# One hybrid decoder layer on one core: queries scaled by minus one eighth on eviction, row minima for row maxima, and a low part cut in eight pieces

## The reference, cut to what matters

```python
    s_own = jnp.einsum('hqd,hld->hql', q_c, k_own).astype(f32) * scale     # scale = ATT_HEAD ** -0.5 = 1/8
    s_own = jnp.where(k_pos[None, None, :] <= q_pos[None, :, None], s_own, NEG_INF)
    p = jax.nn.softmax(jnp.concatenate([s_sel, s_own], axis=-1), axis=-1).astype(v_own.dtype)
...
    merged = (g_a * jnp.einsum('bsc,cd->bsd', y_a, w_br_rwkv[l])
              + g_b * jnp.einsum('bsc,cd->bsd', y_b, w_br_moba[l]))
```

## Time and profile before

| | us |
|---|---|
| median of 3 runs | 1119.45 |
| the runs | 1116.75, 1120.33, 1119.45 |
| profiled execution, its own time | 1114.66 |
| its span | 1112.7 |
| PE busy | 1044.5 (94%) |
| DVE busy | 558.7 (50%) |
| ACT busy | 334.9 (30%) |
| POOL busy | 152.4 (14%) |

### The profile page before, as it was taken

The page is one execution under the profiler, slowest core; times in us unless marked ns, Lnnn a source line. Parts: engine busy times, 40 slices in busy tenths (PEclk is TensorE's granted clock), DMA queues, the critical chain, the costliest instruction groups (busy, mean ns, idle before and its releaser), DMA issues.

```text
span 1112.7 us, 19696 instructions
## 1 busy us (share of the span) xinstructions
PE 1044.5 (94%) x8634; PEld 686.0 (62%) x8634; DVE 558.7 (50%) x883; ACT 334.9 (30%) x567; POOL 152.4 (14%) x168
## 2 busy tenths in 40 slices
PE   4889999999998899999999899999999999999998
PEld 3667799999985678878787434444444444434443
DVE  4648871355547757575566433444333333334334
ACT  6368663033336761322322111111111111111110
POOL 0000000284964430000000100000000000000000
PEclk9899999999999999999999999999999999999999
DMA  9441131000003046466567799999999999999993
GB/s 364 161 152 57 33 115 46 2 14 5 4 8 149 7 163 221 165 225 210 223 249 314 259 406 409 411 398 406 397 406 409 409 407 413 409 406 408 419 417 148
DMA packets 45062, 273.28 MB, mean 246 GB/s; under 512 B 7424, under 2 KB 7568, under 8 KB 31024
## 3 DMA queue, kind: packets, MB, share of 16 engines
q1 hardware_dynamic: 41312, 264.42, 60.4%
q0 software_dynamic: 2656, 4.28, 1.3%
q10 hardware_dynamic: 1008, 3.31, 0.7%
HBM read 271.99 MB, written 4.19 MB: 248 GB/s over the span
## 4 chain that ended last, share of the span: by engine, by line
PE 68%; DMA 22%; DVE 5%; ACT 2%; issue 1%; SPq 1%; DVEq 0%; ACTq 0%; POOLq 0%
PE banks L1611 27%; DMA w_qkv<-in_w 18%; PE banks L2076 13%; PE banks L2090 6%; PE banks L2110 2%; DMA zr<-in_w_ada 2%; PE banks L1763 2%; PE banks L2069 1%; DMA h_table<-w_qkv 1%; PE banks L1765 1%; PE banks L1778 1%; PE banks L2111 1%; PE banks L1923 1%; PE banks L2082 1%; DVE tokm_r L1028 1%
## 5 line engine op out<-in xcount | busy, mean ns | idle before, releaser
L2090 PE MATMUL banks<-w_ring,hidT 128*64 128x512 f32 x512 | 118.6, 606 | 1.0 <-ACT hidT L858 1.0
L1513 DVE TENSOR_TENSOR hid<-banks,silu_a 64x512 f32<-64x512 f32 x32 | 22.2, 693 | 192.3 <-ACT silu_a L854 192.3
L854 ACT ACTIVATE silu_a<-banks 64x512 f32<-64x512 f32 x32 | 18.9, 591 | 272.1 <-PE banks L2077 272.1
L1501 DVE SCALAR_TENSOR_TENSOR mod<-banks,row_weight,mod 64x512 f32<-64x512 f32 x64 | 47.9, 748 | 91.8 <-PE banks L2090 90.8
L944 POOL DMA_INDIRECT picked<-h_table,slot_rows x32 | 29.9, 935 | 419.2 <-PE banks L2069 406.0
L1507 DVE TENSOR_TENSOR x<-x,banks 128x512 f32<-128x512 f32 x120 | 77.1, 684 | 18.5 <-PE banks L2111 18.0
L2076 PE MATMUL banks<-w_ab,xT 128*64 128x512 f32 x176 | 79.2, 604 | 6.2 <-DMA w_tok<-in_w 5.4
L2076 PE MATMUL banks<-w_tok,xT 128*64 128x512 f32 x176 | 77.5, 593 | 5.7 <-DMA w_ring<-in_w 5.7
L2077 PE MATMUL banks<-w_tok,xT 128*64 128x512 f32 x176 | 79.3, 604 | 0.0
L2077 PE MATMUL banks<-w_ring,xT 128*64 128x512 f32 x176 | 77.6, 594 | 0.0
L1611 PE MATMUL banks<-x_r,ring_r 128*128 128x512 f32 x192 | 76.0, 396 | 0.6 <-DVE tokm_r L1028 0.6
(11 more groups left out here) (377 smaller groups left out, 2397.3 us busy)
## 6 DMA issues: line engine op xcount, KB each, us to landing
w_ring<-in_w SPq DMA_DIRECT2D x52, 2048.0 KB, 32.2
w_tok<-in_w SPq DMA_DIRECT2D x22, 2048.0 KB, 30.7
w_ab<-in_w SPq DMA_DIRECT2D x11, 2048.0 KB, 29.8
w_qkv<-in_w SPq DMA_DIRECT2D x10, 2048.0 KB, 35.4
ada_buf<-in_w_ada SPq DMA_DIRECT2D x64, 256.0 KB, 3.1
tokm<-in_w_gate SPq DMA_DIRECT2D x3, 2048.0 KB, 13.2
ring<-in_w_mix SPq DMA_DIRECT2D x5, 1024.0 KB, 5.0
ring<-in_w_ada SPq DMA_DIRECT2D x2, 2048.0 KB, 15.1
```

The lines of the kernel that those rows point to most:

```text
L1501: dve.scalar_tensor_tensor(dst[:, 512 * n:512 * n + 512], bank[5][SLOTS * n:SLOTS * n + SLOTS, :], weight_of(e), gate2[:, n, :], ALU.mult, ...
L1513: dve.tensor_tensor(hid[:, :], bank[3][SLOTS:P, :], silu_a[:, :], ALU.mult).then_inc(hid_v, 1)
L2090: mm = pe.matmul(bank[5][SLOTS * n:SLOTS * n + SLOTS, :], hidT[:, k, :], w2[:, k, 512 * n:512 * n + 512], start=(k == 0), stop=(k == 3))
```

## The change

Four things change. The eviction of the four query banks carries a factor of -1/8 (the four key banks keep 1.0). The mask's entries become +1e30. DVE takes the row minimum of the negated, scaled scores and hands it to ACT directly, so that the multiplication behind the reduction is gone; ACT's exponential takes the factor -1 and that minimum as its bias. POOL's low part of the normed tokens is written in eight instructions of 128x512 in place of two of 128x2048; the semaphore is still raised once for each half, by the last piece of the half.

```diff
-    parts["diag_mask"] = np.where(c <= r, 0.0, NEG)
+    parts["diag_mask"] = np.where(c <= r, 0.0, -NEG)
...
-                act.activation((qT, kT)[j // 4][:, j % 4, :], bank[4 + j % 4][:, :], ACT.Copy).then_inc(qk_a, 1)
+                act.activation((qT, kT)[j // 4][:, j % 4, :], bank[4 + j % 4][:, :], ACT.Copy, scale=(1.0 if j // 4 else -HD ** -0.5)).then_inc(qk_a, 1)
...
-                    act.activation(PROB[u % 2][:, odd, 0:P * (i + 1)], banks[u % 2][:, odd, 0:P * (i + 1)], ACT.Exp, bias=stat[:, at + 2 + odd:at + 3 + odd],
-                                   scale=HD ** -0.5, accum_out=stat[:, at + 4 + odd:at + 5 + odd]).then_inc(exp_a, 1)
+                    act.activation(PROB[u % 2][:, odd, 0:P * (i + 1)], banks[u % 2][:, odd, 0:P * (i + 1)], ACT.Exp, bias=stat[:, at + odd:at + odd + 1],
+                                   scale=-1.0, accum_out=stat[:, at + 4 + odd:at + 5 + odd]).then_inc(exp_a, 1)
...
-                pool.tensor_tensor(h_lo[:, half, :], hT[:, half, :], h_hi[:, half, :].bitcast(f32), ALU.subtract).then_inc(gn_done, 1)
+                for k in range(4 * i, 4 * i + 4):
+                    ins = pool.tensor_tensor(h_lo[:, k, :], hT[:, k, :], h_hi[:, k, :].bitcast(f32), ALU.subtract)
+                ins.then_inc(gn_done, 1)
...
-                seq(dve.reduce_max(stat[:, at:at + 2], banks[u % 2][:, :, 0:P * (tile_of(u) + 1)], AX.X))
-                dve.tensor_scalar(stat[:, at + 2:at + 4], stat[:, at:at + 2], -HD ** -0.5, None, ALU.mult).then_inc(max_v, 1)
+                dve.tensor_reduce(stat[:, at:at + 2], banks[u % 2][:, :, 0:P * (tile_of(u) + 1)], AX.X, ALU.min).then_inc(max_v, 1)
```

## The result

| | before | changed |
|---|---|---|
| median, us | 1116.03 | 1109.44 |
| runs | 6 (1111.99 to 1120.33) | 6 (1106.27 to 1112.07) |
| ratio, 95% interval | | 0.9947 [0.9925, 0.9969] |

The change made the kernel faster by 0.53%, where 0.35% was forecast against the runs shown. The median of before is now 1116.03 us, since three more runs (1115.3, 1111.99, 1113.65) joined the three shown. The profiled execution of the changed kernel took 1112.07 us, with a span of 1110.2 us; it is the slowest of its six.

What follows compares the result with a forecast made beforehand. The attention stage was taken as latency-bound, its chain hopping between engines. Savings of 0.53 + 2.42 + 1.24 = 4.19 us, less POOL's 0.25, gave about 3.9 us off 1119.45: 1115.5 us, range 1112.8 to 1119.2.

Steps and rivals of the forecast that it cites:

- ACT bounds turns 11 to 14, and the gain arrives one to one: Late attention: ACT's own list fills the time; the gain at the first gate product carries whole to the end, chance 0.50.
- the refilled waits: Rival, inside attention: ACT's two idle times partly return because TensorE or scores come late; gain 1.7 us, chance 0.16.
- a gain that doesn't reach the end: Rival, after attention: the weights' stream ends when it did; gain 0 to 1 us, 1119 us, chance 0.10.
- The rival of the slower minimum: Sixteen row reductions: minimum slower than maximum; at twice the time 9.1 us lost, 1128.5 us, chance 0.07.
- The rival of the low clock on dense work: TensorE's 1.2 GHz stretch falls once projections have begun, losing 3 us; gain about 1 us, 1118.5 us, chance 0.17.
- the base of the sum: Whole kernel: the 3.9 us gain was taken from the 1119.45 us median of runs shown, giving 1115.5 us.
- Units 0 to 11: Early attention: 0.31 us at unit 0, 0.11 us each at turns 1 and 3, nothing elsewhere up to turn 10; 0.53 us.
- Turn 11: ACT's idle time ahead of `exps(12)` goes entirely once the multiplication is removed: 2.42 us.
- Turn 13: ACT's idle time ahead of `exps(14)` goes too, if TensorE has the scores in time: 1.24 us.
- The last `sums_out`: End of attention: comes 4.19 us sooner, the sum of 0.53, 2.42 and 1.24 us, from 401.61 to 397.4.
- POOL's tax of 0.25 us: POOL's later finish delays `project(0)`, whose matmuls end at 404.33 instead of the other path's 404.08; 0.25 us taken back.
- The eight pieces thus buy nothing here that I can find: POOL's low part of normed tokens: cutting it adds nothing; the gain is that of the removed multiplication.

Runs made afterwards that it cites:

- The idle POOL: Kernel before, with POOL's low part of the normed tokens done by DVE at the end of attention; 1116.57 us against 1113.3, ratio 1.0023.
- the pieces alone: Kernel before with only POOL's low part of the normed tokens cut into eight pieces, maxima and multiplications kept; 1109.09 us, ratio 0.9947.
- the second comparison: Changed kernel and kernel before measured again, no edit; 1108.08 us over 12 runs against 1114.32 over 23, ratio 0.9946.
- the kernel with the repeated products: Kernel before with unit 10's inverse-sum product done nine times and its value product twice, keeping TensorE busy; 1114.77 us against 1112.17, ratio 1.0023.
- an earlier order of ACT's roundings: Changed kernel with ACT's roundings of branch weights, normed tokens and recurrent output moved to earlier turns, two orders; 1107.47 us (0.9936) and 1108.27 us (0.9948).

## Why the prediction was right in direction and wrong in size

**Right: the mechanism.** The multiplication waited for POOL's running instruction, and its removal took away both idle times of ACT. The idle POOL and the pieces alone showed it from two other sides. The Trainium skill, "SBUF — State Buffer", "Who interferes with whom", has the same: a `tensor_scalar` can take the ports that DVE shares with GpSimd, whoever issued first holds them for the whole instruction, and `tensor_reduce` never contends. The trace agrees: 0.17 us beside an idle POOL, 3.32 to 3.33 us behind a 4.5 us instruction in each of the six profiles of before, and no minimum over 1.23 us beside POOL.

**Right: ACT bounds turns 11 to 14, and the gain arrives one to one.** ACT was busy 5.00 of 5 us, and no stretch behind attention changed clearly but for 0.02 us on the way to the layer input (table above). That refutes, for this kernel, the rivals of the refilled waits and of a gain that doesn't reach the end. The rival of the slower minimum fell with 0.820 against 0.810 us. The rival of the low clock on dense work did not come as described: no drop follows the start of the projections. But the drop ahead of the output projection does fall on dense work and costs 1.6 us where it comes. It took 0.5 ± 0.45 us more from the changed kernel in the mean of six, and is in the kernel before too, so these runs can't tell it from chance. The clock of 0.99 over 184 us doesn't show it.

**Wrong: the base of the sum, "The median of the runs shown, 1119.45, lies 4.8 us above it, and I put it against the median".** This is the step that failed and the larger part of the miss. Three runs gave 1119.45; with three more the median was 1116.03, and 80 further runs beside the experiments had a median of 1113.78. They came in four sets with medians of 1114.32, 1113.3, 1112.17 and 1115.95 us, so the base itself moves by 3.8 us from one set of runs to the next. The other base that the prediction named, the profiled execution's own time, gave 1110.8 us, 1.4 us from the result; no run showed beforehand that it was the better one. Of the 6.1 us between 1115.5 and 1109.44, 3.4 are the base and 2.6 the gain. Of these 2.6, by the table below, 1.0 are terms of the sum that were too small. The other 1.6 us, by which the first comparison's 6.6 lie above 4.95, no stage of the profiles shows. They lie within the comparison's interval, 3.5 to 8.4 us, and I take them for chance between runs, but the second comparison gave 6.2 us, so this stays open.

**Mis-sized: terms of the sum.** By the like-for-like table:

- Units 0 to 11: 0.80 us in place of 0.53. "Elsewhere up to turn 10 it lies beside work of ACT or TensorE; I count nothing" put at nothing what measured 0.27 us.
- Turn 11: 3.41 - 0.80 = 2.61 us in place of 2.42. Where ACT has nothing to wait for, its next instruction starts before the last one's time is over: at 388.63 us behind one of 387.68 + 1.11 = 388.79. The idle time in brackets is counted from that later end and so understates what goes, here by 0.18 us.
- Turn 13: 5.07 - 3.41 = 1.66 us in place of 1.24. From unit 12 to unit 14 took 8.40 to 8.42 us in all profiles of before, though ACT sat idle 1.24 us ahead of unit 14 in the first and 1.43 in the fourth. The first had a second wait, 0.27 us ahead of `sums_out(12)` (1.17 us behind the start of the eviction before it, where the changed kernel has 0.90), which the sum left out. The 0.1 us of the brackets comes to it again.
- The last `sums_out`: 4.94 in place of 4.19, with 0.13 us given back behind unit 14.
- POOL's tax of 0.25 us: absent. The eight pieces took 10.86 us with DVE's instruction among them, where 2 x 5.14 + 1.22 = 11.5 was forecast, and the last four 4.96 in place of 5.14. `project(0)` does wait for POOL, 0.58 us, but its 24 matmuls end at 402.49 + 5.58 = 408.07, and the gate's weights are ready for 408.15. In both kernels the gate product comes 6.66 us behind the last `sums_out`.

The sum is 4.95 us where 3.94 was forecast. The late part, 4.13 us less in six profiles against six, bears most of it out, and so does the mean of the whole distance, 5.25 ± 0.67.

**Half right: "The eight pieces thus buy nothing here that I can find".** Beside the removed multiplication they buy nothing that can be measured (0.9937 without, 0.9946 with). But alone they bring 0.53% themselves and remove the whole stall. The prediction asked only what they add to the other edit, and so did not see that the change holds two cures for one stall.

**Open.** Why the whole gains 6 us in both comparisons and the profiles 4 to 5, why the kernel with the repeated products is 0.23% slower, and whether an earlier order of ACT's roundings gains anything; no kernel tried is distinguishably faster than the changed one.

## What to carry to other kernels

Look at the maximum of a tiny DVE instruction, not at its median: where 0.17 us becomes 3.3, lay its end beside the end of a GpSimd instruction. The cure is either to take the small instruction off DVE's list (fold it into what produces or uses the number) or to cut GpSimd's long instruction into pieces; price each alone, since here they did not add. And take the base of a forecast from as many runs as there are: three runs of this kernel were off by 0.5%, as much as the effect. Where a chance event scatters the whole, compare a part of the way that it doesn't touch: 19.25 and 15.12 us behind unit 11 told in single profiles what medians of twelve runs told only to ±2 us.

## What the hardware showed unexpectedly

- Cutting a GpSimd subtraction of 2048 columns into four cost about 0.5 us: 4.99 and 5.02 us for four, against 4.51 to 4.54 us for one. And DVE gets its turn between two back-to-back pieces: its waits end at the piece's end (392.58 + 1.05 = 393.63 against 393.62).
- The reciprocal of 128x2 took 0.15 to 0.17 us everywhere, also beside a running GpSimd instruction (391.51 in the changed kernel), where the multiplication of the same shape waited.
- In attention, where TensorE works with gaps, its clock fell to half for some 3 us at places that differ between executions of one program; each time cost 1.1 to 1.5 us. Behind one and the same wait of 2.02 us ahead of the output projection it fell in four executions of twelve, at 1.6 us each. The time was lost only where TensorE was waited for: the same drop behind the stall cost nothing.
